# The token vector of the expert dots is read from two PSUM banks for three of the four token tiles; the merge and latent-head stages give up two PSUM banks each

## The chip, the cores and the metric

The kernel runs on one core of a Trainium2 chip. The metric is the device time of one execution in microseconds (us). The engines are named as in the profile: PE is TensorE (its weight loads are PEld), DVE is VectorE, ACT is ScalarE, POOL is GpSimd, SP is SyncE, which here only issues DMAs.

## The reference

Two transformer blocks over 512 tokens of width 1024. The first has a Mamba-2 scan, a short convolution, a merge of the two and a layer of 16,384 small experts; the second has two kinds of attention and an MLP. The expert layer is the part that the change touches:

```
def peer_ffn(h, w_q, sub_keys, expert_u, expert_v):
...
        u = expert_u[eidx]
        v = expert_v[eidx]
        act = jax.nn.gelu(jnp.einsum('td,thkd->thk', xb, u).astype(jnp.float32), approximate=False)
        return jnp.einsum('thk,thkd->td', (g * act).astype(v.dtype), v)
```

`eidx` holds 8 heads x 16 chosen experts per token. Per token, 128 rows of `peer_u` are each multiplied with the token's vector and summed (a dot), the 128 dots go through a gelu, and 128 rows of `peer_v`, each times its coefficient, are added up.

## The kernel before

The 512 tokens are four tiles of 128 tokens (one token on each of the 128 partitions), handled as two halves of two tiles. Block one (`project`, `scan`, `merge`, norm, `route`) runs for the first half and then for the second; block two (`mix_two`, `mlp_two`) follows. A stage ends when PE, DVE, ACT and SP have arrived at its barrier.

The experts are background work in class `Experts`. There are 1024 units in a fixed order: for each tile 128 dot units, then 128 add units. One unit is one row gather of 128 rows of 4 KB, one per token, 0.52 MB:

- POOL issues it (`indirect_dma_start`, L1254). It reads the 128 row numbers from the SBUF tile `chosen`, and the rows land in one of the 16 slots of the ring `expert_rows`. Before it issues unit n, POOL waits until unit n-16 has been used.
- A dot unit is used by DVE in one instruction (L1328): slot times token vector `u`, written back to the slot, with the sum along the row as accumulator output. Both inputs lie in SBUF.
- An add unit is used by DVE (L1338, slot times coefficient plus `h` or `u`), or, for some of them (`tensor_units`), by PE: a matmul with a diagonal matrix that adds up in the two PSUM banks `expert_sum` (L1288); DVE adds these to `h` at the tile's end (L1352).

Each foreground stage has a quota of units (`PLAN_ONE`, `PLAN_TWO`). DVE takes some between its own instructions (`bg.use`) and the rest of the quota after its last instruction of the stage (`bg.use_rest`), so a late gather holds up what stands behind it on DVE. Which tile runs where:

- dots of the first tile: `project` of the second half; its adds: `scan` of the second half
- dots of the second tile: `merge` of the second half, 54 of them at its start, then 6 or 4 after each DVE step; its adds: the end of `merge`, the norm, `route`
- dots of the third tile: norm, `project_two` (all 72 of its quota in `use_rest`, since DVE has nothing else there), `latent_heads` and the start of `attend`; its adds: `attend` to the first `norm_add`
- fourth tile: what follows, to the end of its adds in the first `mlp_two`

Weights come in slabs of 2 MB that SP loads into two buffers; the load of a slab waits until PE has used the one that lay there.

PSUM has eight banks. `expert_sum` is held in `scan`, `route` and from `attend` on. In `merge` four banks `y_turned` take first the transposes of y, then the gate products; ACT empties them. In `latent_heads` three banks `lat_turned` take transposes.

Of the kernel before, what the change touches and what calls it, by code (L numbers as in the profile page):

```python
# [15 lines left out]
ds = bass.ds  # L16
# [91 lines left out]
def _program(nc, t, out, top):  # L108
# [268 lines left out]
    with first:  # L377
# [38 lines left out]
        def block_one(half, buffers, lend, bg, plans):  # L416
# [56 lines left out]
            with ExitStack() as ctx:  # L473
# [20 lines left out]
        bg.start(0, u[0], part_h[0], chosen[0], weight[0], chosen_ready)  # L494
        block_one(1, [uT[:, i, 0:META + TOK - SC_TAPS + 1] for i in range(7)],
                  (part_h[1], tiles_of(u1[:])), bg, PLAN_ONE + (UNITS,))
        bg.start(1, u1, part_h[1], chosen1, weight1, chosen_ready)
# [6 lines left out]
    def mix_two(first, T, seen, now, plan, per, prepared=None):  # L504
# [4 lines left out]
        with ExitStack() as ctx:  # L509
# [38 lines left out]
            landed = [sem(f"out2_landed{i}", keep=True) for i in range(2)]  # L548
            if now and first == 0:
                now.share_with_tensor(ctx, psum)  # L550
            plan()
# [45 lines left out]
    with ExitStack() as ctx:  # L597
        plans = iter(PLAN_TWO + (2 * UNITS,))
        plan = lambda: bg.plan(next(plans))
        LAST = TT + 1  # L600
        seen = [keys_and_values(ctx)]
        with experts:
            mix_two(0, TT, seen, bg, plan, 3)
# [22 lines left out]
def project(frame, slab_loader, ident, uT, z, xs, xs_meta, bt, bt_meta, bf, cf, dt, constants, carry,  # L626
# [10 lines left out]
    with ExitStack() as ctx:  # L637
# [6 lines left out]
        turned = [psum(ctx, f"x_turned{i}", [P, NT, P]) for i in range(2)]  # L644
        turned_meta = [psum(ctx, f"x_turned_meta{i}", [P, 512]) for i in range(2)]
        dt_bank = turned[0][:].rearrange("p t c -> p (t c)")[:, 0:(TT + 1) * HEADS].rearrange(
# [274 lines left out]
def scan(frame, consts, z, xs, xs_meta, bt, bt_meta, bf, cf, dt, decays, state, rows, half, bg, scaling, gating=None):  # L921
# [12 lines left out]
    with ExitStack() as ctx:  # L934
# [8 lines left out]
        root, scale, root_ready, y_scaled = scaling  # L943
        if bg:
            bg.share_with_tensor(ctx, psum)
        sums = psum(ctx, "sums", [P, 512])
# [240 lines left out]
class Experts:  # L1187
# [15 lines left out]
    def __init__(self, nc, t, sem, ctx, block, ident):  # L1203
# [12 lines left out]
        self.tensor_units += [UNITS + n for n in range(SLOTS + 8, TO_ATTENTION) if n % 8 in self.IN_ATTENTION]  # L1216
        self.halves = []
        self.goal = self.done = self.active = self.diags = self.products = self.sums = self.base = 0

# [59 lines left out]
    def tensor_sums(self, pe, n):  # L1279

        end = self.by_tensor(min(self.base + n, self.goal))
        for k in range(self.products, end):
# [4 lines left out]
            for side in range(2):  # L1287
                ins = pe.matmul(self.total[side][:], self.diag[:, k % self.DIAGS, :],  # L1288
                                self.row(unit)[:, side * 512:(side + 1) * 512],
                                start=k == self.by_tensor(tile), stop=k == self.by_tensor(tile + SLOTS) - 1)  # L1290
# [49 lines left out]
    def _sum_up(self, dve, end, u, h):  # L1340
# [4 lines left out]
        if shared:  # L1345
# [4 lines left out]
            for side in range(2):  # L1350
                o = h[:, side * 512:(side + 1) * 512]
                ins = dve.tensor_tensor(o, o, self.total[side][:], ALU.add)  # L1352
        ins.then_inc(self.complete, 1)
# [6 lines left out]
def merge(frame, ident, uT, z, yT, gates, vT, h, small, half, bg, y_scaled, slab, landed, loaded):  # L1360
# [7 lines left out]
    with ExitStack() as ctx:  # L1368
# [54 lines left out]
        def _(pe):  # L1423
            enter(pe)
            def turn_y():

                pe.wait_ge(y_scaled, TT)
                for j in range(KI):
                    if j >= 4:
                        pe.wait_ge(turned_used, j - 3)  # L1430
                    for m in range(TT):
                        ins = pe.transpose(turned[j % 4][:, 0, m * P:(m + 1) * P], z[:, m, j * P:(j + 1) * P], ident[:])
                    ins.then_inc(turned_done, 1)
# [4 lines left out]
            for i in range(0, 2 if own_gates else 0):  # L1438
                for s in range(2):
                    pe.wait_ge(landed[s], i * 16 + 16)  # L1440
                    for q in range(2):
                        pe.wait_ge(gates_used, i * 4 + (2 * s + q + 1))
                        for j in range(2):
                            c = (2 * q + j) * P
                            for k in range(KD):
                                ins = pe.matmul(turned[2 * s + q][:, j, :], slab[s][:, k, c:c + P], uT[:, k, own],
                                                start=k == 0, stop=k == KD - 1)
# [49 lines left out]
        def _(act):  # L1497
# [3 lines left out]
            def drain_y():  # L1501
                for j in range(KI):
                    act.wait_ge(turned_done, j + 1)
                    act.activation(yT[:, j, :], turned[j % 4][:, 0, :], ACT.Copy,
                                   scale=gain[:, j:j + 1]).then_inc(turned_used, 1)
# [3 lines left out]
            for i in range(0, 2 if own_gates else 0):  # L1509
                for p_ in range(4):  # L1510
                    act.wait_ge(product, i * 4 + (p_ + 1))
                    act.activation(gates[i][:, ds(2 * p_, 2), :], turned[p_][:], ACT.Sigmoid
                                   ).then_inc(gates_used, 1)
# [79 lines left out]
def route(frame, slab_loader, ident, uT, slab, chosen, weight, room, count, bg,  # L1593
# [8 lines left out]
    with ExitStack() as ctx:  # L1602
# [19 lines left out]
        at = kept("best_at_float").bitcast(BF16)[:, 0:Q * TOPK]  # L1622
        if bg:
            bg.share_with_tensor(ctx, psum)
        product = [psum(ctx, f"q_product{i}", [P, 512]) for i in range(2)]
# [334 lines left out]
def latent_heads(frame, ident, eps, small, constants_in, latent, qbT, kbT, values, first, T, bg):  # L1960
# [10 lines left out]
    with ExitStack() as ctx:  # L1971
# [34 lines left out]
        def _(act):  # L2006
# [11 lines left out]
            for j in range(3):  # L2018
                act.wait_ge(turned_done, j + 1)
                act.activation(latT[:, j, :], lturn[j][:, 0:T, :].rearrange("p m c -> p (m c)"), ACT.Copy,  # L2020
                               scale=gain[:, j:j + 1]).then_inc(latT_ready, 1)
            act.wait_ge(reduced, 1)
# [90 lines left out]
        def _(pe):  # L2113
            enter(pe)
            pe.wait_ge(scaled, 2 * T)
            for j in range(3):
                for m in range(T):
                    ins = pe.transpose(lturn[j][:, m, :], normed[:, m, j, :], ident[:])
                ins.then_inc(turned_done, 1)
# [984 lines left out]
```

## Time and profile before

| | |
|---|---|
| device time, median of 3 runs | 2778.02 us (2776.9 to 2784.32) |
| span of the profiled execution, first to last instruction | 2853.2 us |
| the profiled execution's device time | not recorded apart from its span |
| busy: PE / DVE / POOL / ACT | 2357.0 / 1754.3 / 1247.8 / 576.5 us |
| DMA | 832.08 MB, mean 292 GB/s; 536.94 MB of it by POOL's gathers (q0) |

Busy times are sums of instruction durations. The POOL time is nearly all from the 1024 gather issues: an issue is busy on POOL until its descriptors are made, and the transfer itself comes later. The profiled execution was 75.2 us longer than the median run; durations and order are read from it, the time itself from the runs.

### The profile page before, as it was taken

To read this page: it belongs to the slowest core of one execution; us is meant where nothing else is said; L and a number is where in the kernel's file an instruction comes from. 1 tells how busy PE (TensorE), PEld (TensorE's weight loads), DVE (VectorE), ACT (ScalarE), POOL (GpSimd) and SP (SyncE) were. 2 spreads that over 40 slices of the span, in tenths; PEclk is the share of its full clock that TensorE was granted. 3 is DMA by queue.
4 is the path that set the end of the run, shared out by engine and by line. 5 is a ranking of instruction groups with operands and counts; after the bars stand their busy time and mean duration, and the time that the engine had idled before them with its cause. 6 is when DMAs were issued, how large, how long until landed. Compare 5 with 4: busy or idle time off the path is not lost. (4 is left out here: it accounts for less than half of the span.)

```text
span 2853.2 us, 28354 instructions
## 1 busy us (share of the span) xinstructions
PE 2357.0 (83%) x9768; PEld 1658.2 (58%) x9768; DVE 1754.3 (61%) x3620; ACT 576.5 (20%) x1562; POOL 1247.8 (44%) x1058
## 2 busy tenths in 40 slices
PE   7999999889774887799788766486497799999988
PEld 6847888565662555588454454234185455557765
DVE  3325420179998887486768876975868677741510
ACT  4421300111332221000112201231123211012321
POOL 0000000004887666477545576675566577710000
PEclk9998999999996888899899887698796899999999
DMA  4322243337999999999987999898899899973376
GB/s 153 148 105 79 97 150 145 140 118 305 411 412 322 364 360 379 363 403 415 415 323 245 332 364 365 318 354 319 347 414 380 327 414 414 414 284 126 130 282 227
DMA packets 187055, 832.08 MB, mean 292 GB/s; under 512 B 22417, under 2 KB 22673, under 8 KB 174113
## 3 DMA queue, kind: packets, MB, share of 16 engines
q0 software_dynamic: 147456, 536.94, 49.0%
q1 hardware_dynamic: 39456, 293.33, 26.3%
q8 instruction: 79, 1.29, 0.2%
q14 instruction: 64, 0.52, 0.1%
HBM read 828.09 MB, written 2.10 MB: 291 GB/s over the span
## 5 line engine op out<-in xcount | busy, mean ns | idle before, releaser
L1254 POOL DMA_INDIRECT expert_rows<-in_peer_u,chosen x512 | 660.0, 1289 | 985.2 <-DVE chosen L1839 641.0
L1254 POOL DMA_INDIRECT expert_rows<-in_peer_v,chosen x512 | 584.4, 1141 | 275.8 <-issue 140.7
L1328 DVE SCALAR_TENSOR_TENSOR expert_rows<-expert_rows,u 128x1024 f32<-128x1024 f32 x512 | 603.2, 1223 | 69.8 <-DMA expert_rows<-in_peer_u,chosen 43.8
L1338 DVE SCALAR_TENSOR_TENSOR h<-expert_rows,expert_coef,h 128x1024 f32<-128x1024 f32 x194 | 249.9, 1288 | 34.3 <-DMA expert_rows<-in_peer_v,chosen 26.2
L1338 DVE SCALAR_TENSOR_TENSOR u<-expert_rows,expert_coef,u 128x1024 f32<-128x1024 f32 x190 | 244.9, 1289 | 38.5 <-DMA expert_rows<-in_peer_v,chosen 32.5
L1288 PE MATMUL expert_sum<-expert_rows,expert_diag 128*128 128x512 f32 x496 | 241.6, 634 | 30.1 <-ACT expert_diag L1275 21.9
L2977 PE MATMUL mlp_up<-mlp_xT,mlp_slab 128*128 128x384 f32 (+1 forms) x1024 | 227.4, 384 | 1.3 <-ACTq L132 0.8
L2969 PE MATMUL mlp_down<-mlp_slab,upT 128*128 128x512 f32 x512 | 222.2, 592 | 0.0
L2977 PEld LDWEIGHTS mlp_up<-mlp_xT,mlp_slab 128*128 128x128 f32 x1024 | 158.1, 195 | 73.6 <-issue 5.7
L1288 PEld LDWEIGHTS expert_sum<-expert_rows,expert_diag 128*128 128x128 f32 x496 | 95.7, 203 | 137.9 <-issue 132.0
L2969 PEld LDWEIGHTS mlp_down<-mlp_slab,upT 128*128 128x128 f32 x512 | 96.7, 190 | 117.1 <-issue 115.3
L720 PE MATMUL product<-uT,expert_rows 128*128 128x272 f32 x512 | 121.5, 393 | 0.8 <-DMA expert_rows<-in_w_in 0.8
L720 PE MATMUL product<-uT,in_slab 128*128 128x256 f32 x512 | 114.6, 379 | 0.0
L1902 PE MATMUL in_product<-xT,in_slab 128*128 128x256 f32 x320 | 80.3, 400 | 38.4 <-issue 38.2
L720 PEld LDWEIGHTS product<-uT,expert_rows 128*128 128x128 f32 x512 | 95.3, 190 | 19.4 <-DVEq L132 0.9
L720 PEld LDWEIGHTS product<-uT,in_slab 128*128 128x128 f32 x512 | 95.4, 190 | 12.4 <-issue 0.5
L815 DVE SCALAR_TENSOR_TENSOR h<-h,conv_taps 128x272 f32<-128x272 f32 x96 | 48.2, 502 | 80.1 <-ACT h L788 77.9
L1902 PEld LDWEIGHTS in_product<-xT,in_slab 128*128 128x128 f32 x320 | 63.7, 200 | 55.3 <-issue 47.5
L3001 ACT ACTIVATE upT<-mlp_up 128x384 f32<-128x384 f32 (+1 forms) x64 | 24.6, 384 | 334.3 <-PE mlp_up L2977 321.7
L1456 PE MATMUL mix_product<-uT,expert_rows 128*128 128x258 f32 (+1 forms) x384 | 85.4, 386 | 5.1 <-ACTq L132 5.1
L1456 PE MATMUL mix_product<-uT,mix_slab 128*128 128x258 f32 (+1 forms) x384 | 84.0, 381 | 0.5 <-DVE u L1556 0.5
L1456 PEld LDWEIGHTS mix_product<-uT,expert_rows 128*128 128x128 f32 x384 | 74.1, 193 | 16.0 <-ACTq L132 5.2
(559 smaller groups left out, 3604.0 us busy)
## 6 DMA issues: line engine op xcount, KB each, us to landing
expert_rows<-in_w_in SPq DMA_DIRECT2D x27, 2048.0 KB, 7.4
in_slab<-in_w_in SPq DMA_DIRECT2D x22, 2048.0 KB
mlp_slab<-in_w_up SPq DMA_DIRECT2D x64, 512.0 KB, 6.1
mlp_slab<-in_w_down SPq DMA_DIRECT2D x64, 512.0 KB, 5.3
mix_slab<-in_w_in SPq DMA_DIRECT2D x10, 2048.0 KB
out_slab<-in_w_out SPq DMA_DIRECT2D x6, 2048.0 KB, 7.9
expert_rows<-in_ssd_w_out SPq DMA_DIRECT2D x4, 2048.0 KB, 8.0
expert_rows<-in_peer_w_q SPq DMA_DIRECT2D x4, 2048.0 KB, 9.7
```

The costliest lines, as they stand in the source:

```text
L720: ins = pe.matmul(bank[n % 4][:, 0:W], slab[s][:, k, c:c + P], uT[:, k, A:A + W], start=k == 0, stop=k == KD - 1)
L815: ins = dve.scalar_tensor_tensor(a, b[:, k:k + W], taps[:, n, k:k + 1], a, ALU.mult, ALU.add)
L1254: pool.indirect_dma_start(out=self.row(n), out_offset=None, in_=self.tables[0 if dot else 1], in_offset=bass.IndirectOffsetOnAxis(ap=picks ...
L1288: ins = pe.matmul(self.total[side][:], self.diag[:, k % self.DIAGS, :], self.row(unit)[:, side * 512:(side + 1) * 512], start=k == self.by ...
L1328: dve.scalar_tensor_tensor(self.row(n), self.row(n), 1.0, u, ALU.mult, ALU.mult, accum_out=dot).then_inc(self.rows_used, 1)
L1338: dve.scalar_tensor_tensor(o, self.row(n), coef, o, ALU.mult, ALU.add).then_inc(self.rows_used, 1)
L1456: ins = pe.matmul(pair[r % 2][:, j, 0:w], lhs(j, k), rhs(k), start=k == 0, stop=k == k_tiles - 1)
L1902: ins = pe.matmul(both[n % 4][:, j, :], lhs(j, k), xT[:, k, :], start=k == 0, stop=k == KD - 1)
L2969: ins = pe.matmul(down[2 * m + side][:], upT[:, n % (2 * PER), m * P:(m + 1) * P], as_down(i % R)[:, j, side * 512:(side + 1) * 512], star ...
L2977: ins = pe.matmul(bank[n % UPS][:, 0:W], slab[i % R][:, j, k, :], xT[:, k, :], start=k == 0, stop=k == KD - 1)
L3001: act.activation(o, bank[n % UPS][:, 0:W], ACT.Relu).then_inc(relu_done, 1)
```

## The change

- `expert_sum` becomes one PSUM tile of two banks. As before PE sums into its halves. In addition, as `near`, it holds the token vector of the tile whose dots are taken.
- At the first dot of a tile DVE copies `u` there (`_bring`: it waits until its own earlier uses have ended, copies, waits for the copy). The dots read `near` in place of `u`.
- The two banks are held through the whole second half of block one, and through the first `mix_two` (`share_with_tensor`); after that `end_share` sets `near` to None, and the fourth tile's dots read `u` in SBUF as before.
- `project` allocates its meta banks in the first half alone; `merge` in the second half has two `y_turned` banks in place of four; `latent_heads` packs its first two transposed tiles in one bank, and ACT waits for both before it reads the first.

```
+        with ExitStack() as ctx:
+            bg.share_with_tensor(ctx, psum)
+            block_one(1, ...)
...
+            with ExitStack() as shared:
+                bg.share_with_tensor(shared, psum)
+                mix_two(0, TT, seen, bg, plan, 3)
+            bg.end_share()
...
     def share_with_tensor(self, ctx, psum):
-        self.total = [psum(ctx, f"expert_sum{i}", [P, 512]) for i in range(2)]
+        both = psum(ctx, "expert_sum", [P, 2, 512])
+        self.total = [both[:, side, :] for side in range(2)]
+        self.near, self.held = both[:].rearrange("p a n -> p (a n)"), None
...
             if dot:
-                self._dot(dve, n, u[:, m, :], self.coef[:, m, at:at + 1])
+                if self.near is not None and self.held != (half, m):
+                    self._bring(dve, n, u[:, m, :])
+                    self.held = half, m
+                self._dot(dve, n, u[:, m, :] if self.near is None else self.near, self.coef[:, m, at:at + 1])
...
+    def _bring(self, dve, n, u):
+        if self.by_vector(n):
+            dve.wait_ge(self.rows_used, self.by_vector(n))
+        dve.tensor_copy(self.near, u).then_inc(self.brought, 1)
+        self.brings += 1
+        dve.wait_ge(self.brought, self.brings)
...
-        turned = [psum(ctx, f"y_turned{i}", [P, 2, TOK]) for i in range(4)]
+        TURNED = 2 if bg else 4
+        turned = [psum(ctx, f"y_turned{i}", [P, 2, TOK]) for i in range(TURNED)]
...
-                    if j >= 4:
-                        pe.wait_ge(turned_used, j - 3)
+                    if j >= TURNED:
+                        pe.wait_ge(turned_used, j - TURNED + 1)
...
-                        pe.wait_ge(gates_used, i * 4 + (2 * s + q + 1))
+                        n = i * 4 + 2 * s + q
+                        pe.wait_ge(gates_used, 4 - TURNED + n + 1)
...
-        lturn = [psum(ctx, f"lat_turned{i}", [P, NT, P]) for i in range(3)]
+        turned_two = [psum(ctx, f"lat_turned{i}", [P, 2, T * P]) for i in range(2)]
+        lturn = [turned_two[j // 2][:, j % 2, :] for j in range(3)]
...
-                act.wait_ge(turned_done, j + 1)
+                act.wait_ge(turned_done, 2 if j < 2 else 3)
```

DVE at the start of `project` of the second half, before (`expert_coef` is where a dot's sum goes):

```order
L801 UNCONDITIONAL_BRANCH
L1328 SCALAR_TENSOR_TENSOR expert_rows,expert_coef<-expert_rows,u 128x1024 x12
L815 SCALAR_TENSOR_TENSOR uT<-uT,conv_taps 128x256 x3
L1328 SCALAR_TENSOR_TENSOR expert_rows,expert_coef<-expert_rows,u 128x1024 x3
L815 SCALAR_TENSOR_TENSOR uT<-uT,conv_taps 128x256 x3
```

The same place in the changed kernel:

```order
L804 UNCONDITIONAL_BRANCH
L1340 COPY expert_sum<-u 128x1024
L1347 SCALAR_TENSOR_TENSOR expert_rows,expert_coef<-expert_rows,expert_sum 128x1024 x12
L818 SCALAR_TENSOR_TENSOR uT<-uT,conv_taps 128x256 x3
L1347 SCALAR_TENSOR_TENSOR expert_rows,expert_coef<-expert_rows,expert_sum 128x1024 x3
L818 SCALAR_TENSOR_TENSOR uT<-uT,conv_taps 128x256 x3
```

One copy is new, and the dots name `expert_sum` (PSUM) where they named `u` (SBUF); number and order are the same. Two more copies stand at the start of `merge` of the second half and in the norm at the start of the first `mix_two`.

PE in `merge` of the second half, at the change from the transposes of y to the gate products, before:

```order
L1432 MATMUL y_turned_340<-ident,z 128x128 x2
L1432 MATMUL y_turned_341<-ident,z 128x128 x2
L1446 MATMUL y_turned_338<-uT,mix_slab_331 128x256 x16
L1446 MATMUL y_turned_339<-uT,mix_slab_331 128x256 x16
L1446 MATMUL y_turned_340<-uT,mix_slab_332 128x256 x16
L1446 MATMUL y_turned_341<-uT,mix_slab_332 128x256 x16
```

and in the changed kernel:

```order
L1452 MATMUL y_turned_336<-ident,z 128x128 x2
L1452 MATMUL y_turned_337<-ident,z 128x128 x2
L1468 MATMUL y_turned_336<-uT,mix_slab_329 128x256 x16
L1468 MATMUL y_turned_337<-uT,mix_slab_329 128x256 x16
L1468 MATMUL y_turned_336<-uT,mix_slab_330 128x256 x16
L1468 MATMUL y_turned_337<-uT,mix_slab_330 128x256 x16
```

The same work goes through two banks by turns instead of four.

## Rows read from the trace of the kernel before

**Rows 1.** The page: costliest POOL and DVE groups; busy us, mean ns, idle before

```profile
L1254 POOL DMA_INDIRECT expert_rows<-in_peer_u,chosen x512 | 660.0, 1289 | 985.2 <-DVE chosen L1839 641.0
...
L1328 DVE SCALAR_TENSOR_TENSOR expert_rows<-expert_rows,u 128x1024 f32<-128x1024 f32 x512 | 603.2, 1223 | 69.8 <-DMA expert_rows<-in_peer_u,chosen 43.8
```

**Rows 2.** Timeline, POOL, dots back to back: start, us, engine, line, op

```profile
867.14 1.98 POOL L1254 DMA_INDIRECT expert_rows<-in_peer_u,chosen  x1 [0.30 <-issue]
```

**Rows 3.** Timeline, DVE, the same place

```profile
865.95 1.22 DVE L1328 SCALAR_TENSOR_TENSOR expert_rows<-expert_rows,u 128x1024 f32<-128x1024 f32 x1
...
867.09 1.22 DVE L1328 SCALAR_TENSOR_TENSOR expert_rows<-expert_rows,u 128x1024 f32<-128x1024 f32 x1
```

**Rows 4.** Timelines of DVE and POOL, 1226 to 1227 us

```profile
1226.25 0.68 DVE L1556 TENSOR_TENSOR u<-u,mix_product 128x512 f32<-128x512 f32 x1
...
1226.30 0.94 POOL L1254 DMA_INDIRECT expert_rows<-in_peer_u,chosen  x1 [0.30 <-issue]
```

**Rows 5.** Stretches: length, busy PE PEld DVE ACT POOL; PE clock, DMA share, GB/s

```profile
715.00:857.00 142.00, 105.86 (x508) 87.87 (x508) 139.51 (x260) 46.12 (x137) 115.17 (x89) 0.95 1.02 413
857.00:880.00 23.00, 0.00 (x0) 0.00 (x0) 22.82 (x42) 1.79 (x2) 19.65 (x12) 0.50 0.85 280
...
1611.00:1660.00 49.00, 42.00 (x170) 31.29 (x171) 44.20 (x80) 12.82 (x28) 36.29 (x23) 0.86 0.88 313
1660.00:1740.00 80.00, 41.59 (x143) 29.77 (x142) 61.84 (x103) 4.27 (x6) 61.59 (x56) 0.68 1.02 407
1690.00:1730.00 40.00, 9.86 (x17) 4.79 (x17) 30.68 (x51) 0.00 (x0) 30.30 (x29) 0.50 1.02 412
...
1825.00:1925.00 100.00, 74.08 (x233) 35.19 (x233) 78.95 (x158) 38.73 (x138) 77.11 (x67) 0.81 0.96 356
```

**Rows 6.** Timeline, PE, the end of `project_two`

```profile
1734.07 32.32 PE L1902 MATMUL in_product<-xT,in_slab 128*128 128x256 f32 x140 [0.63 <-issue]
```

**Rows 7.** Timeline, PE, `merge` of the second half after its gate products

```profile
1184.98 41.82 PE L1456 MATMUL mix_product<-uT,mix_slab 128*128 128x258 f32 x192
...
1355.67 29.20 PE L1490 MATMUL mix_product<-mix_slab,z 128*128 128x512 f32 x64 [2.86 <-DVE z L1575]
```

**Rows 8.** Groups of DVE and ACT instructions: busy us, mean ns, idle before

```profile
L1344 DVE TENSOR_TENSOR h<-h,u 128x1024 f32<-128x1024 f32 x4 | 4.9, 1225 | 0.1
...
L293 DVE TENSOR_SCALAR mix_normed<-x_in,mix_scale 128x1024 f32<-128x1024 f32 x4 | 3.0, 754 | 0.1
...
L1575 DVE TENSOR_TENSOR u<-u,gated 128x512 f32<-128x512 f32 x4 | 2.8, 691 | 0.1
...
L1572 DVE TENSOR_TENSOR gated<-h,mix_product 128x512 f32<-128x512 f32 x4 | 2.7, 687 | 22.7 <-PE mix_product L1456 22.7
...
L1504 ACT ACTIVATE yT<-y_turned,ssd_gain 128x256 f32<-128x256 f32 x16 | 6.3, 489 | 5.7 <-PE y_turned L1432 5.7
```

**Rows 9.** DVE's waits, 857 to 895 us: total, times, longest

```profile
DVE u L1336 <- DMA expert_rows<-in_peer_v,chosen: 2.8, 1, 2.8
DVE expert_rows L1328 <- DMA expert_rows<-in_peer_u,chosen: 1.2, 2, 0.8
DVE h L1338 <- DMA expert_rows<-in_peer_v,chosen: 0.8, 1, 0.8
```

**Rows 10.** The dots of 1602 to 1767 us, and the idle time ahead of them

```profile
L1328 DVE SCALAR_TENSOR_TENSOR expert_rows<-expert_rows,u x92: 1210/1224/1295, 1611.1 to 1749.2; 128x1024 f32<-128x1024 f32 x92
...
  DMA expert_rows<-in_peer_u,chosen: 17.9, 10
  issue: 4.0, 9
```

**Rows 11.** DVE's waits, 1801 to 1963 us (`attend`)

```profile
DVE u L1338 <- DMA expert_rows<-in_peer_v,chosen: 7.8, 6, 2.3
...
DVE h L1338 <- DMA expert_rows<-in_peer_v,chosen: 3.2, 3, 1.6
```

**Rows 12.** DMA queue of the weight slabs, 1240 to 1300 us: packets, MB, share

```profile
q1 hardware_dynamic: 576, 8.39, 33.1%
```

More of the change, by code:

```diff
@@ L494, in _program @@
         bg.start(0, u[0], part_h[0], chosen[0], weight[0], chosen_ready)
-        block_one(1, [uT[:, i, 0:META + TOK - SC_TAPS + 1] for i in range(7)],
-                  (part_h[1], tiles_of(u1[:])), bg, PLAN_ONE + (UNITS,))
+        with ExitStack() as ctx:
+            bg.share_with_tensor(ctx, psum)
+            block_one(1, [uT[:, i, 0:META + TOK - SC_TAPS + 1] for i in range(7)],
+                      (part_h[1], tiles_of(u1[:])), bg, PLAN_ONE + (UNITS,))
         bg.start(1, u1, part_h[1], chosen1, weight1, chosen_ready)
@@ L548, in mix_two @@
             landed = [sem(f"out2_landed{i}", keep=True) for i in range(2)]
-            if now and first == 0:
-                now.share_with_tensor(ctx, psum)
             plan()
@@ L644, in project @@
         turned = [psum(ctx, f"x_turned{i}", [P, NT, P]) for i in range(2)]
-        turned_meta = [psum(ctx, f"x_turned_meta{i}", [P, 512]) for i in range(2)]
+        turned_meta = [psum(ctx, f"x_turned_meta{i}", [P, 512]) for i in range(2)] if M else None
         dt_bank = turned[0][:].rearrange("p t c -> p (t c)")[:, 0:(TT + 1) * HEADS].rearrange(
@@ L943, in scan @@
         root, scale, root_ready, y_scaled = scaling
-        if bg:
-            bg.share_with_tensor(ctx, psum)
         sums = psum(ctx, "sums", [P, 512])
@@ L1217, in __init__ @@
         self.halves = []
+        self.near, self.brought, self.brings = None, sem("tokens_in_psum", keep=True), 0
         self.goal = self.done = self.active = self.diags = self.products = self.sums = self.base = 0
@@ L1263, in share_with_tensor, with end_share @@
     def share_with_tensor(self, ctx, psum):
-        self.total = [psum(ctx, f"expert_sum{i}", [P, 512]) for i in range(2)]
+        both = psum(ctx, "expert_sum", [P, 2, 512])
+        self.total = [both[:, side, :] for side in range(2)]
+        self.near, self.held = both[:].rearrange("p a n -> p (a n)"), None
+    def end_share(self):
+        self.near = None
     def diagonals(self, act, n):
@@ L1287, in tensor_sums @@
             for side in range(2):
-                ins = pe.matmul(self.total[side][:], self.diag[:, k % self.DIAGS, :],
+                ins = pe.matmul(self.total[side], self.diag[:, k % self.DIAGS, :],
                                 self.row(unit)[:, side * 512:(side + 1) * 512],
@@ L1351, in _sum_up @@
                 o = h[:, side * 512:(side + 1) * 512]
-                ins = dve.tensor_tensor(o, o, self.total[side][:], ALU.add)
+                ins = dve.tensor_tensor(o, o, self.total[side], ALU.add)
         ins.then_inc(self.complete, 1)
@@ L1428, in turn_y @@
                 for j in range(KI):
-                    if j >= 4:
-                        pe.wait_ge(turned_used, j - 3)
+                    if j >= TURNED:
+                        pe.wait_ge(turned_used, j - TURNED + 1)
                     for m in range(TT):
-                        ins = pe.transpose(turned[j % 4][:, 0, m * P:(m + 1) * P], z[:, m, j * P:(j + 1) * P], ident[:])
+                        ins = pe.transpose(turned[j % TURNED][:, 0, m * P:(m + 1) * P], z[:, m, j * P:(j + 1) * P],
+                                           ident[:])
                     ins.then_inc(turned_done, 1)
@@ L1445, in _ @@
                             for k in range(KD):
-                                ins = pe.matmul(turned[2 * s + q][:, j, :], slab[s][:, k, c:c + P], uT[:, k, own],
+                                ins = pe.matmul(turned[n % TURNED][:, j, :], slab[s][:, k, c:c + P], uT[:, k, own],
                                                 start=k == 0, stop=k == KD - 1)
@@ L1503, in drain_y @@
                     act.wait_ge(turned_done, j + 1)
-                    act.activation(yT[:, j, :], turned[j % 4][:, 0, :], ACT.Copy,
+                    act.activation(yT[:, j, :], turned[j % TURNED][:, 0, :], ACT.Copy,
                                    scale=gain[:, j:j + 1]).then_inc(turned_used, 1)
@@ L1511, in _ @@
                     act.wait_ge(product, i * 4 + (p_ + 1))
-                    act.activation(gates[i][:, ds(2 * p_, 2), :], turned[p_][:], ACT.Sigmoid
+                    act.activation(gates[i][:, ds(2 * p_, 2), :], turned[p_ % TURNED][:], ACT.Sigmoid
                                    ).then_inc(gates_used, 1)
@@ L1622, in route @@
         at = kept("best_at_float").bitcast(BF16)[:, 0:Q * TOPK]
-        if bg:
-            bg.share_with_tensor(ctx, psum)
         product = [psum(ctx, f"q_product{i}", [P, 512]) for i in range(2)]
@@ L2018, in _ @@
             for j in range(3):
-                act.wait_ge(turned_done, j + 1)
-                act.activation(latT[:, j, :], lturn[j][:, 0:T, :].rearrange("p m c -> p (m c)"), ACT.Copy,
-                               scale=gain[:, j:j + 1]).then_inc(latT_ready, 1)
+                act.wait_ge(turned_done, 2 if j < 2 else 3)
+                act.activation(latT[:, j, :], lturn[j], ACT.Copy, scale=gain[:, j:j + 1]).then_inc(latT_ready, 1)
             act.wait_ge(reduced, 1)
@@ L2117, in _ @@
                 for m in range(T):
-                    ins = pe.transpose(lturn[j][:, m, :], normed[:, m, j, :], ident[:])
+                    ins = pe.transpose(lturn[j][:, m * P:(m + 1) * P], normed[:, m, j, :], ident[:])
                 ins.then_inc(turned_done, 1)
```

1 line of the change is left out of this document (removed).

## The prediction

> **What bounds the kernel now.** I read the page first. No engine is busy all through: DVE has 61% of the span, and its costliest group is the dots; ahead of them it sat idle 69.8 us, 43.8 of that for gathered rows that had not landed. A gather's issue keeps POOL 1289 ns on average in the dots' half [rows 1]. That average is worth opening, so the timelines of POOL and DVE came next, where dots run back to back. An issue that starts at 867.14, 0.05 us into a dot, takes 1.98 us. The dot ends at 868.31, the issue at 869.12, 0.81 us later [rows 2, 3]. Dots follow each other every 1.14 us [rows 3], issues every 1.98 + 0.30 = 2.28 us, so one gather passes per two dots. The counter-example is an issue that starts 0.05 us into a DVE instruction which reads one operand from PSUM (`mix_product`) and the other from SBUF and writes SBUF: it takes 0.94 us [rows 4]. The reader is to see that the issue is held until a dot with two SBUF inputs has ended, and that 0.94 us is its own length.
>
> The Trainium skill, "SBUF — State Buffer", section "Who interferes with whom", says as much: a DVE instruction with two SBUF inputs contends with a GpSimd instruction that reads SBUF. The trace agrees (1.98 against 0.94 us).
>
> Next, where does a held issue cost anything? The stretches tell. In 715 to 857 us DVE is busy 139.5 of 142 us and the DMA engines move 413 GB/s: both are full, and quicker issues have nowhere to go. In 857 to 880 us it is 280 GB/s, in 1611 to 1660 us 313 GB/s, with POOL busy on 23 issues for 36.3 us. After that, 1660 to 1740 us, it is 407 GB/s again [rows 5]. I take 413 GB/s as a full DMA. In `merge` PE is the bound: from 1184.98 its matmul runs follow one another to 1384.9 (1355.67 + 29.20) with next to no gap, at most 2.86 us [rows 7], so DVE's waits there are paid from PE's slack.
>
> One stretch needs care. In 1690 to 1730 us PE has 17 records in 40 us, at half clock (0.50, 1.2 GHz), with the DMA full at 412 GB/s [rows 5]; the profile doesn't say why. At the pace of `merge`, 41.82 us for 192 records [rows 7], 17 records take 3.7 us, so some 36 us are stall. The profiled span is 75.2 us longer than the median run, so the timed runs can't hold all such stalls. PE ends `project_two` at 1766.4 in the profile [rows 6]; without 36 us of it that is 1730, ahead of the last dot of that quota at 1749.2 [rows 10]. In the timed runs I therefore take DVE, waiting for gathers, as what ends that stage. This is my choice; the profile alone says PE.
>
> **The change part by part.** The sum is of differences, and is taken from the median run, 2778.0; against the profile's span the same sum gives 2853.2 minus it, with `project_two` then in doubt.
>
> Dots themselves: 384 of 512 read PSUM. At 128x512 an instruction with one PSUM input takes 687 ns, one with both in SBUF 691 ns [rows 8]. I take 0 per dot.
>
> The Trainium skill, "VectorE: DVE Perf Modes", section on the TRN2 errata, speaks against the change: a fixed cost of 120 cycles from PSUM against 58 from SBUF, 62 cycles or 0.065 us at 0.96 GHz. By it the 384 dots would take an estimated 25 us more; rows 8 show nothing of the kind.
>
> Three copies of 128x1024 into PSUM: none is in the trace. Nearest are 754 ns (one input, SBUF to SBUF) and 1225 ns (two inputs) [rows 8]. PSUM as the output makes me take the upper one, with 0.1 for the two semaphore waits: 1.3 us. The first stands in `project`, where DVE is full, the third in the norm ahead of `project_two`, where PE waits for DVE: both are on the path. The second stands before 54 dots of `merge`, covered by PE's slack; without that cover it would be 1.3 more. Cost 2.6, between 1.5 and 4.
>
> Fewer banks: transposes in `merge` are paced by ACT's 16 copies of 489 ns [rows 8] with four banks or two; a gate product is 16 matmuls with two records each, 32 x 41.82/192 = 7.0 us [rows 7], far longer than ACT needs to empty a bank. `latent_heads` makes ACT wait for one more pair of transposes. Together 1 us, 0 to 2.
>
> End of the first tile's dots (857 to 895 us): DVE uses the last 23 dots back to back with POOL held on nearly each, uses up its lead, and then waits 2.8 + 1.2 + 0.8 = 4.8 us [rows 9]. With issues every 0.94 + 0.30 = 1.24 us against a dot every 1.14 the lead stays. What stands behind is the scan's own start on DVE. I take 3 gained, 0 to 4.8.
>
> Dots of the second tile (`merge`): PE-bound, 0, from 3 lost to 4 gained.
>
> Dots of the third tile (norm and `project_two`): 23 issues in 36.3 us would take 21.6. The DMA moved 313 GB/s in place of 413 for 49 us, a lack of 49 x (1 - 313/413) = 11.9 us [rows 5]. After it the DMA is full, so that this is all that can be given back, although DVE's waits sum to 17.9 + 4.0 = 21.9 us [rows 10]. I take 10, 0 to 12.
>
> Start of `attend`: the tile's last dots are still taken here, and the adds behind them run at 356 GB/s, not DMA-bound, with issues of 77.11/67 = 1.15 us on average [rows 5]. Adds have two SBUF inputs as before, so they go on holding POOL. But POOL comes to them with a fuller ring, and that can pay for part of DVE's waits of 7.8 + 3.2 = 11.0 us [rows 11]. I take 5, 0 to 11.
>
> The fourth tile isn't touched. Its adds end inside the first MLP.
>
> Sum: 3 + 10 + 5 - 2.6 - 1 = 14.4 us. **2778.0 - 14.4 = 2764 us.**
>
> **The rivals.**
> A, the issues get short, but the time is hidden. In the timed runs PE ends `project_two` after DVE, as in the profile, or the DMA is full a little later and nothing comes through: only the 3 us of 857 to 895 remain against 3.6 of cost, 2779 us. For it: PE's end at 1766.4, and 407 to 413 GB/s wherever the DMA was not starved. Against: the 75 us that the profile has too much.
> B, slower: the weight slabs pay. While gathers are queued, the slab queue gets 8.39 MB in 60 us, 140 GB/s [rows 12], so that a slab of 2.1 MB takes 15.0 us; PE uses one in 64 records, a third of the 192 in 41.82 us: 13.9 us [rows 7]. Today the gather queue thins out whenever POOL is held, and slabs catch up. If it never does, each of the 14 slabs from 1185 to 1385 us costs PE 1.1 us: 15 us, and with the other stages' gain lost 2778 + 15 + 3.6 - 3 = 2794 us. It decides once PE waits for slabs in more than that stage's odd tile. Against: the number of gathers per stage is fixed, and at 1240 to 1300 us the queues were full already while PE did not wait.
> C, a dot from PSUM is longer than one from SBUF. At 0.037 us per dot (14.4/384) the gain is gone, if all of it is on the path; at 0.05 us it is 19 us, 2783 us. Against: 687 against 691 ns, though these have half the length and no accumulator.
> D, the issue is held by the dot's write to SBUF or its accumulator, not by the second input; then only costs remain, 2782 us. Against: the instruction of rows 4 writes SBUF too. The Trainium skill's same SBUF section infers that making descriptors needs the write side alone, so that an instruction with two inputs wouldn't hold it; the trace disagrees, as shown.
>
> **How the numbers follow.** Forecast 0.60, A 0.22, B 0.10, C 0.05, D 0.03. A measurement of this kernel tells about 0.3%, 8.3 us, from no change. The forecast's own range runs from all upper gains at the lowest cost (4.8 + 4 + 12 + 11 - 1.5 = 30 us) to a small one, 2748 to 2775. Faster than 2769.7: 0.56 of the forecast, 0.03 of A. Slower than 2786.3: B's 0.10, 0.02 of C, 0.01 of D. The rest, 0.28, lies within. The range reaches from 2742, a little under the upper gains for a stage whose timed course I don't see, to 2784, which takes in A, C and D and leaves out B.
>
> **What would show it.** Issues in the dots of the first three tiles at 0.94 us, and as long as before in the fourth tile's; dots at 1.22; three copies between 0.75 and 1.3 us; over 390 GB/s where 280 and 313 stood; DVE's waits for `in_peer_u` rows before the fourth tile shorter. The forecast is wrong if PE shows waits for slabs in `merge` or `project_two` (B), if dots lengthen (C), if issues stay at 1.98 (D), or if all this comes out as said and the stages end when they did (A).

## The result and the profile after

| | before | after |
|---|---|---|
| device time, median | 2777.46 us (2774.11 to 2784.32, 4 runs) | 2752.68 us (2749.13 to 2757.73, 4 runs) |
| ratio after / before | | 0.9906, 95% interval 0.9885 to 0.9926 |
| span of the profiled execution | 2853.2 us | 2748.2 us, its device time 2750.07 |

The change gains 24.8 us; the forecast was 14.4. Timed again beside the later experiments the ratio was 0.9917 (0.9903 to 0.993). The profiled execution of after took 2.6 us less than the median of its runs, that of before 75 us more. A difference of these two profiles, 105 us, is therefore no measure of the change, and a second profile of the kernel before was taken first; what is compared below is that one (span 2775.4 us), unless the text says the first.

The page of after, costliest groups of POOL and DVE (busy us, mean ns, idle before), answers to [rows 1]:

```profile
L1256 POOL DMA_INDIRECT expert_rows<-in_peer_u,chosen x512 | 529.9, 1035 | 1040.9 <-DVE chosen L1859 640.5
...
L1347 DVE SCALAR_TENSOR_TENSOR expert_rows<-expert_rows,expert_sum 128x1024 f32<-128x1024 f32 x384 | 451.8, 1217 | 77.2 <-DMA expert_rows<-in_peer_u,chosen 72.4
...
L1347 DVE SCALAR_TENSOR_TENSOR expert_rows<-expert_rows,u 128x1024 f32<-128x1024 f32 x128 | 151.7, 1225 | 24.0 <-DMA expert_rows<-in_peer_u,chosen 17.3
```

A gather's issue in the dots' half is 0.25 us shorter on average than in the first profile of before (0.23 us than in the second, 1261 ns), and a dot from PSUM takes 1217 ns beside 1225 from SBUF in the same kernel. Back-to-back dots near 865 us, the place that [rows 2, 3] showed, POOL's timeline and then DVE's (start, us):

```profile
864.72 0.93 POOL L1256 DMA_INDIRECT expert_rows<-in_peer_v,chosen  x1 [0.30 <-issue]
865.96 0.94 POOL L1256 DMA_INDIRECT expert_rows<-in_peer_v,chosen  x1 [0.30 <-DVE expert_rows L1347]
```

```profile
864.72 1.22 DVE L1347 SCALAR_TENSOR_TENSOR expert_rows<-expert_rows,expert_sum 128x1024 f32<-128x1024 f32 x1
865.86 1.22 DVE L1347 SCALAR_TENSOR_TENSOR expert_rows<-expert_rows,expert_sum 128x1024 f32<-128x1024 f32 x1
```

Both issues start in the first 0.1 us of a dot, take 0.93 and 0.94 us, and end before the dot does. Of the 296 issues that start inside a dot of the first three tiles (inside means that the dot is what DVE began last) the longest takes 0.95 us. The like-for-like comparison is with issues that start in the first 0.3 us of such a dot: before, 93 of 106 take over 1 us, and the median of the 106 is 1.98; after, none of 95 does. The 83 inside dots of the fourth tile, which read `u` in SBUF, still go up to 1.99.

The three copies, in the answer for line 1340 (ns, least, median, most):

```profile
L1340 DVE COPY expert_sum<-u x3: 1220/1227/1228, 685.6 to 1561.7; 128x1024 f32<-128x1024 f32 x3
```

### The profile page after: what moved, and what is told of

Its sections match the earlier page's. It is cut to its first block and busy times, and to the rows that moved or that the text cites. A ratio compares the mean times of both kernels' runs of the same rounds, so it can differ in the third digit from the quotient of the medians.

```text
span 2748.2 us, 28360 instructions
## 1 busy us (share of the span) xinstructions
PE 2328.0 (85%) x9768; PEld 1645.1 (60%) x9768; DVE 1756.2 (64%) x3623; ACT 576.9 (21%) x1562; POOL 1102.6 (40%) x1058
## 5 line engine op out<-in xcount | busy, mean ns | idle before, releaser
L1256 POOL DMA_INDIRECT expert_rows<-in_peer_u,chosen x512 | 529.9, 1035 | 1040.9 <-DVE chosen L1859 640.5
L1256 POOL DMA_INDIRECT expert_rows<-in_peer_v,chosen x512 | 569.3, 1112 | 260.9 <-issue 126.6
L1347 DVE SCALAR_TENSOR_TENSOR expert_rows<-expert_rows,expert_sum 128x1024 f32<-128x1024 f32 x384 | 451.8, 1217 | 77.2 <-DMA expert_rows<-in_peer_u,chosen 72.4
L1296 PE MATMUL expert_sum<-expert_rows,expert_diag 128*128 128x512 f32 x496 | 235.1, 619 | 23.5 <-ACT expert_diag L1283 17.7
L1347 DVE SCALAR_TENSOR_TENSOR expert_rows<-expert_rows,u 128x1024 f32<-128x1024 f32 x128 | 151.7, 1225 | 24.0 <-DMA expert_rows<-in_peer_u,chosen 17.3
L1478 PEld LDWEIGHTS mix_product<-uT,mix_slab 128*128 128x128 f32 x384 | 75.8, 198 | 19.8 <-DVE sc_sx L1560 4.0
```

What stands on the lines that cost most here:

```text
L1256: pool.indirect_dma_start(out=self.row(n), out_offset=None, in_=self.tables[0 if dot else 1], in_offset=bass.IndirectOffsetOnAxis(ap=picks ...
L1296: ins = pe.matmul(self.total[side], self.diag[:, k % self.DIAGS, :], self.row(unit)[:, side * 512:(side + 1) * 512], start=k == self.by_te ...
L1347: dve.scalar_tensor_tensor(self.row(n), self.row(n), 1.0, u, ALU.mult, ALU.mult, accum_out=dot).then_inc(self.rows_used, 1)
L1478: ins = pe.matmul(pair[r % 2][:, j, 0:w], lhs(j, k), rhs(k), start=k == 0, stop=k == k_tiles - 1)
```

## The experiments

**1. The kernel before, profiled again.**

> The kernel before, unchanged, so that a second profile of it exists. Theory 1 (the first profile of it held stalls that the timed runs don't have): the span comes out near the timed median, 2770 to 2785 us, project_two of the first mix is 20 to 45 us shorter than its 145.5 us there, and the records of TensorE between 1690 and 1730 us don't thin out. Its idle time before the dots of tile three, 21.9 us, stays. Rival: the profiler always lengthens this kernel, then the span is again 2830 to 2870 us, although the changed kernel's profile had 2748.2 us against a median of 2752.7. Time: 1.000 times itself, within 0.3%.

Measured: 2776.72 us, ratio to itself 1.0003 (0.999 to 1.0017), span 2775.4. The first profile was long by 78 us: 25 in `scan` and 16 in `route` of the second half, 46 in `project_two`, of which `latent_heads` gave 32 back (the dots had caught up in the stall), 11 in `attend`, and about 3 in each of three others. Why is open; no later profile was like it. The timeline of PE and the stretches of before, second profile (length, busy PE PEld DVE ACT POOL; PE clock, DMA share, GB/s):

```profile
1659.66 12.47 PE L1902 MATMUL in_product<-xT,in_slab 128*128 128x256 f32 x57
1709.33 1.51 PE L2118 MATMUL lat_turned<-ident,latent_normed 128*128 128x128 f32 x6 [37.21 <-DVE latent_normed L2046]
```

```profile
1576.00:1626.00 50.00, 50.00 (x194) 38.26 (x194) 39.24 (x68) 5.21 (x10) 41.46 (x29) 0.92 0.87 298
1626.00:1672.00 46.00, 46.00 (x214) 40.28 (x212) 32.35 (x53) 3.58 (x6) 32.65 (x34) 1.00 1.02 415
```

and the same of after:

```profile
1659.72 11.82 PE L1922 MATMUL in_product<-xT,in_slab 128*128 128x256 f32 x54
1694.30 1.51 PE L2138 MATMUL lat_turned<-ident,latent_normed 128*128 128x128 f32 x6 [22.76 <-DVE latent_normed L2066]
```

```profile
1576.00:1626.00 50.00, 50.00 (x191) 38.04 (x191) 48.59 (x87) 5.21 (x10) 37.79 (x41) 0.92 1.02 411
1626.00:1672.00 46.00, 45.54 (x211) 39.74 (x210) 34.31 (x57) 4.01 (x7) 27.74 (x30) 1.00 1.02 414
```

This is the main reading of the case. The stall of PE in `project_two` [rows 5] is gone from both kernels: PE works through to 1672 us in each, busy for all of the first 50 us, so `project_two` ends when it did, and nothing is gained in it. The third tile's dots run beside it. With issues held, 29 pass in 50 us and the DMA moves 298 GB/s; unheld, 41 pass and it moves 411. What is behind comes out where PE first needs DVE again, at the transposes of `latent_heads`: PE sat idle 37.21 us ahead of them, and now 22.76, 14.5 us less. DVE gets to them only after its rest of the quota of `project_two`, which it uses after it has arrived at that stage's barrier (at 1591.5 us before, at 1590.2 after). The first of DVE's own instructions behind that rest, before and then after:

```profile
1707.93 0.17 DVE L2042 RECIPROCAL latent_scale<-latent_root 128x4 f32<-128x4 f32 x1
```

```profile
1692.73 0.17 DVE L2062 RECIPROCAL latent_scale<-latent_root 128x4 f32<-128x4 f32 x1
```

As expected were the span, a shorter `project_two` (by 46 us, where 20 to 45 was expected), PE's records, and that DVE's waits for rows of tile three stay: 23.2 us up to the end of `project_two`, 26.4 in all, where 21.9 had been up to the end of that stage.

The lengths of the stages of the second half and of the first mix, each from the last arrival at one barrier to the last arrival at the next, from the traces of before and after:

| | before | after | difference |
|---|---|---|---|
| `project` | 225.1 | 224.9 | -0.2 |
| `scan` | 212.7 | 207.6 | -5.1 |
| `merge` | 286.6 | 286.8 | 0.2 |
| `route` | 183.0 | 187.7 | 4.7 |
| `project_two` | 99.3 | 99.9 | 0.6 |
| `latent_heads` | 66.0 | 50.3 | -15.7 |
| `attend` | 150.7 | 138.4 | -12.2 |
| all the rest | 1551.7 | 1552.4 | 0.7 |

**2. What holds the issue: the write, or the second input?** First the banks of the changed kernel without its copies; every dot reads `u` in SBUF, and every second one writes to PSUM:

```
+        to_psum = self.near is not None and n % 2
+        if to_psum and self.by_vector(n) > 1:
+            dve.wait_ge(self.rows_used, self.by_vector(n) - 1)
-        dve.scalar_tensor_tensor(self.row(n), self.row(n), 1.0, u, ALU.mult, ALU.mult,
+        dve.scalar_tensor_tensor(self.near if to_psum else self.row(n), self.row(n), 1.0, u, ALU.mult, ALU.mult,
                                  accum_out=dot).then_inc(self.rows_used, 1)
```

> Banks as in the changed kernel, no copies, dots with both inputs in SBUF; in the first three tiles every second dot (the odd ones) writes its product, which nobody reads, to the two PSUM banks and not to the slot. Theory (the issue of a gather is held by the second SBUF input): issues that start inside either kind of dot last as long as before, up to 1.98 us, median 1.5 to 1.7, and end 0.81 us after the dot. Rival D (it is held by the write to SBUF): issues that start inside a dot that writes PSUM take 0.94 us, and only those inside the even dots are held.

Measured: 2776.42 us in one run beside 2775.56 of before. Timelines of DVE and POOL in this kernel:

```profile
689.79 1.23 DVE L1347 SCALAR_TENSOR_TENSOR expert_sum<-expert_rows,u 128x1024 f32<-128x1024 f32 x1
```

```profile
689.84 1.99 POOL L1256 DMA_INDIRECT expert_rows<-in_peer_u,chosen  x1 [0.30 <-issue]
```

The issue starts 0.05 us into a dot that writes PSUM and is held just as long, 1.99 us. Of 122 issues that start inside such dots 76 take over 1 us and end 0.80 us behind the dot; the median of all 122 is 1.62 us. Rival D falls for the write.

The second half of the question, with one SBUF input and the write left in SBUF (this kernel leaves out the product with `u`, so its dots have other values; gathers and order are the same):

```
-        dve.scalar_tensor_tensor(self.row(n), self.row(n), 1.0, u, ALU.mult, ALU.mult,
-                                 accum_out=dot)
+        dve.tensor_scalar(self.row(n), self.row(n), 1.0, 0.0, ALU.mult, ALU.add, accum_out=dot)
```

> The kernel before, with every dot replaced by an instruction with one SBUF input (slot times 1.0 plus 0.0, written back, with the accumulator output): the product with u is left out, no PSUM bank is touched by it. Theory (the second SBUF input holds the issue): all issues inside these take 0.94 us, those inside adds stay up to 1.98. Rival (an accumulator output, or a write to SBUF, holds it): up to 1.98 us as before. The time says little, since such an instruction may be shorter than a dot, 0.75 to 1.22 us.

The instruction turned out as long as a dot, so its time says more than expected: 2748.84 us, one run. The same two timelines:

```profile
863.23 1.21 DVE L1328 TENSOR_SCALAR_CACHE_REDUCE expert_rows<-expert_rows 128x1024 f32<-128x1024 f32 x1
```

```profile
863.26 0.94 POOL L1254 DMA_INDIRECT expert_rows<-in_peer_v,chosen  x1 [0.30 <-issue]
```

None of 383 issues inside these takes over 0.96 us, though they write SBUF and have an accumulator. `latent_heads` takes 50.5 us and `attend` 140.1, as in the changed kernel. So PSUM adds nothing of its own that these runs show; what counts is that one SBUF input is gone.

**3. Only the banks, and banks with copies.** In the first the call of `_bring` is taken out and the dots read `u`; in the second the copies are made and the dots read `u`:

```
-                self._dot(dve, n, u[:, m, :] if self.near is None else self.near, self.coef[:, m, at:at + 1])
+                self._dot(dve, n, u[:, m, :], self.coef[:, m, at:at + 1])
```

> The changed kernel with its banks (sharing, two banks less in merge and in latent_heads), but without the copies and with dots that read u in SBUF. Theory (the gain is the second SBUF input): the time of before, 2775 to 2781 us, fewer banks costing 0 to 2 us; issues inside dots as long as before. Rival (the gain comes from the banks or from where things lie): 2752 to 2765 us.

> The same, with the three copies made, but dots that still read u in SBUF. Theory: the copies cost 2.6 us over the kernel with the banks alone, between 1.5 and 4: 2777 to 2784 us. Each copy lasts 1.1 to 1.3 us. If a copy lasts 0.75 us, their cost is under 2 us and not to be told from nothing.

Measured: 2776.92 us, ratio 1.0007 (0.9994 to 1.002), and 2773.86 us, ratio 1.0001 (0.9987 to 1.0014). Neither can be told from the kernel before; the copies, 3.7 us of DVE time by their durations, are lost in the scatter of a median. Issues inside dots still go up to 1.99 us in both. The gain is in the operand. (In `latent_heads` the change gives up one bank, three to two, not two as the title and the expectation have it; `merge` gives up two.)

**4. One tile at a time.** `near` is used for one tile's dots alone:

```
+                near = self.near if (half, m) == (0, 0) else None
-                if self.near is not None and self.held != (half, m):
+                if near is not None and self.held != (half, m):
```

with (0, 1) for the second tile and (1, 0) for the third.

> The changed kernel, but with the copy and the PSUM operand for the dots of the first tile alone; the other dots read u in SBUF. Theory as forecast: scan of the second half ends earlier by 3 to 5 us (5.1 in the two profiles), less 1.2 of copy; merge is bound by TensorE and keeps that. Revised by the second profile of before: route gives these 5 us back (TensorE starts it at a lower clock), and the end of project_two is the same to 0.6 us, so 2773 to 2778 us. Rival (the first tile carries the gain through fuller rings): 2755 to 2765 us.

> The same for the dots of the second tile alone, which run in merge of the second half. Theory: TensorE bounds merge, 0 us, from 3 lost to 4 gained around the time of the kernel with the banks alone: 2773 to 2780 us, merge 286 to 288 us. Rival B (slabs pay while the gather queue is never thin): merge 290 to 300 us and the time above 2785 us.

> The same for the dots of the third tile alone. Theory: nearly the whole gain is here, 2750 to 2757 us, with latent_heads some 15 us and attend some 12 us shorter than the 66.0 and 150.7 us in the second profile of before. Rival (all three tiles share the gain as in the forecast, 3 of 18 us in the first): 2755 to 2765 us, with attend shorter by 5 us at most.

| PSUM operand for | median | ratio to before (95%) |
|---|---|---|
| first tile | 2773.84 us | 0.9989 (0.9976 to 1.0002) |
| second tile | 2780.54 us | 1.0007 (0.9993 to 1.0022) |
| third tile | 2756.17 us | 0.9926 (0.9902 to 0.9949) |
| all three (the change, timed again) | 2752.56 us | 0.9917 (0.9903 to 0.993) |

The third tile carries the gain, 21.8 us by its medians (20.6 by its ratio) of the 24.2 to 24.8 of the whole change. With the second tile alone `merge` takes 285.7 us, so rival B does not appear there. PE's timelines at the first transposes of `latent_heads`, third tile alone and then first tile alone:

```profile
1706.36 1.51 PE L2139 MATMUL lat_turned<-ident,latent_normed 128*128 128x128 f32 x6 [23.06 <-DVE latent_normed L2067]
```

```profile
1714.44 1.51 PE L2139 MATMUL lat_turned<-ident,latent_normed 128*128 128x128 f32 x6 [38.25 <-DVE latent_normed L2067]
```

With the third tile alone `latent_heads` takes 50.3 us and `attend` 139.7, with the first alone 66.8 and 144.6. The first tile gives 3 us by its ratio (7 to -1 by the interval), nothing that is certain: its own profile has `scan` at 214.9 us, longer than before. Over all kernels of this study `scan` of the second half took 207.5 to 216.4 us in no order (the first profile's 237.8 left out), so the 5.1 us of the table are within its scatter.

The same holds for a part of the 12.2 us of `attend`. Here are all profiles that have the quotas of before, again without the first, by what the third tile's dots read. Two SBUF inputs: the kernel before, the two of experiment 3, the one that writes PSUM, first tile alone, second tile alone. One: the changed kernel (twice), third tile alone, the one-input kernel of experiment 2.

| | two SBUF inputs, 6 profiles | one SBUF input, 4 profiles | difference of the means |
|---|---|---|---|
| `project_two` | 95.9 to 99.8, mean 98.6 | 97.6 to 99.9, mean 99.2 | 0.6 |
| `latent_heads` | 63.7 to 67.1, mean 65.6 | 50.3 to 52.5, mean 50.9 | -14.7 |
| `attend` | 144.6 to 151.2, mean 148.4 | 135.3 to 140.1, mean 138.4 | -10.0 |

In `latent_heads` and `attend` the two groups don't overlap. The means give 24.1 us, close to the 24.8 of the timed runs; the one pair of profiles gave 27.3 in the same stages.

**5. The quotas.** PE still waits 22.76 us for DVE in `latent_heads`. So 12 units of `project_two` were moved behind it, in both kernels to `merge_two`, and in the changed one also to `attend` instead:

```
-PLAN_TWO = (20, 72, 22, 86, 48, 8, 8, 36, 24, 10, 4, 3)
+PLAN_TWO = (20, 60, 22, 86, 60, 8, 8, 36, 24, 10, 4, 3)     to merge_two
+PLAN_TWO = (20, 60, 22, 98, 48, 8, 8, 36, 24, 10, 4, 3)     to attend
```

> The changed kernel, unchanged, timed beside the two below. 2748 to 2758 us, ratio 0.989 to 0.993. Its profile again has latent_heads at 50 us and attend at 138 to 140 us; scan of the second half anywhere from 207 to 216 us if its 5.1 us were scatter, 207 to 209 us if they belong to the change.

> The changed kernel with 12 units of the quota of project_two given to merge_two (72 and 48 become 60 and 60). Theory: DVE's rest of that quota, which runs on after TensorE has ended project_two, is what ends latent_heads, and merge_two has 26 us of idle DVE at its end: latent_heads 12 to 15 us shorter (12 dots of 1.22 to 1.28 us), some of it given back in attend, 2738 to 2745 us. Rival (TensorE's own work of latent_heads or the slabs end it once DVE is 5 us earlier, or attend takes all of it back): 2748 to 2755 us.

> The same quotas in the kernel before. Theory: it gains as much, 12 to 15 us, 2762 to 2768 us, and stays some 20 us behind the changed kernel with these quotas, since its dots still hold POOL. Rival (what the operand gives and what the quota gives are the same idle time of TensorE in latent_heads): it gains more than the changed kernel does, 20 us or over, and comes within 10 us of it.

> The changed kernel with 12 units of project_two's quota given to attend instead of merge_two (72 and 86 become 60 and 98). The sum of the first four quotas stays 200, so TensorE keeps its share of the third tile's adds, which it lost with the other plan. Theory: latent_heads 13.6 us shorter as there, DVE's 9.2 us of idle time at the start of merge_two pays for most of the units, and norm_add stays at 15.6 us: 2736 to 2743 us. Rival (VectorE has no such slack, whatever the stage the units are put in): 2744 to 2752 us.

| kernel | median | ratio to before (95%) |
|---|---|---|
| changed | 2752.56 us | 0.9917 (0.9903 to 0.993) |
| changed, 12 units to `merge_two` | 2745.51 us | 0.9893 (0.9878 to 0.9908) |
| changed, 12 units to `attend` | 2751.99 us | 0.9908 (0.9888 to 0.9928) |
| before, 12 units to `merge_two` | 2770.72 us | 0.998 (0.997 to 0.999) |

The changed kernel, profiled again here, has `latent_heads` at 52.5 us and `attend` at 135.3 (50 and 138 to 140 were expected) and `scan` at 207.5, which leaves open whether those 5.1 us are more than scatter.

PE at the transposes in the changed kernel with 12 units in `merge_two`:

```profile
1677.22 1.51 PE L2138 MATMUL lat_turned<-ident,latent_normed 128*128 128x128 f32 x6 [6.46 <-DVE latent_normed L2066]
```

`latent_heads` lost 13.6 us as expected, but about half came back. The expectation had taken DVE's arrival at the barrier of `merge_two`, 26 us ahead of PE's, for idle time. It is none: DVE goes on there with its rest of the quota. DVE's waits from 1895 to 1950 us show its one idle stretch in the changed kernel:

```profile
DVE post_mix_scale L2881 <- ACT post_mix_root L2869: 9.3, 1, 9.3
```

It is absent from the answer for the kernel with 12 units in `merge_two`, whose `norm_add` is 5.4 us longer: DVE makes 67 adds from `merge_two` to there instead of 54, since fewer adds fall to PE too. With the units in `attend` that stage is 8.6 us longer and `merge_two` 5.6, and of the 13.7 next to nothing is left; there the expectation missed altogether, and the rival held. DVE's busy time in `attend` had risen by 13 us (115.69 to 128.98). It looks as if DVE is the bound, or close to it, from `latent_heads` to `norm_add`. The kernel before gained 6 us from the same move, no more than the changed one, so that the two gains do not compete; the 12 to 15 us expected of it were missed for the same reason, with `latent_heads` 14.3 us shorter (51.7) and `norm_add` 6.8 longer (22.4). Best of the study by the median is the changed kernel with 12 units in `merge_two`, 7 us ahead of the changed one beside it; the intervals of their ratios just overlap.

## Why the forecast was right in kind and short in size

**Dots cost nothing from PSUM: right.** 1217 against 1225 ns. Rival C had no part. The larger fixed cost from PSUM that the Trainium skill states (page "VectorE: DVE Perf Modes", section on the TRN2 errata), by the prediction's estimate 0.065 us per dot, does not appear in these instructions, of which one input is in PSUM and the other in SBUF.

**The issue is held by a second SBUF input: right, and now shown** by experiments 2, one that moves the write away and one that takes the input away. The rule of the Trainium skill, "SBUF — State Buffer", section "Who interferes with whom", agrees with 0.94 against up to 1.99 us, also while the write is elsewhere, if the issue counts as an instruction that reads SBUF; its rows name `chosen`, the SBUF tile of the row numbers, as an input. The prediction went too far in saying that the trace disagrees with the page's inference that making descriptors needs only the write side: what is held may be the reading of the row numbers, and no run here separates the two.

**Copies 2.6 and banks 1: right as far as can be told.** A copy takes 1.23 us (1.3 taken). Of the 3.6 us taken for both, the kernel with both (experiment 3) shows somewhere between 3.9 us lost and 3.6 gained, by its interval.

**First tile, 3 (0 to 4.8): not settled.** Alone it gave 3 us, with an interval from 1 lost to 7 gained. The waits of 4.8 us [rows 9] were those of the first profile. In the second they are 1.6 us, so that there was less to give back:

```profile
DVE h L1338 <- DMA expert_rows<-in_peer_v,chosen: 1.0, 1, 1.0
DVE u L1336 <- DMA expert_rows<-in_peer_v,chosen: 0.6, 1, 0.6
```

**Second tile, 0: right.** `merge` is 286.6 and 286.8 us, DVE's waits for rows there 57.3 and 57.5 us, on PE's slack both times. Rival B had no part either: PE shows no wait for a slab there, nor in `project_two`.

**Third tile, 10 (0 to 12): the first term that was too small,** 14.7 measured as a mean (15.7 in the pair of profiles), above its upper bound. The forecast took the lack of bytes from 49 us that begin with the tile's first dot, 49 x (1 - 313/413) = 11.9 us, as the most that could come back. In the second profile the first dot is at 1563.0, and the starved stretch is from 1576 to 1626, deeper since the full queue of the first 13 us isn't in it: 50 x (1 - 298/413) = 13.9 us, and PE's idle time fell by 14.5. And the place was wrong: "in the timed runs I therefore take DVE, waiting for gathers, as what ends that stage". The order was right: DVE's last dot of that quota ends at 1707.9 us, PE at 1672.1. But the stage doesn't wait for these dots, since DVE arrived at the barrier at 1591.5 and used the rest behind it. So PE ends `project_two`, as rival A had it, but A's conclusion that the time is then hidden did not follow: DVE's rest runs on past the barrier and holds up PE in `latent_heads` instead.

**Start of `attend`, 5 (0 to 11): the second,** 10.0 measured as a mean, twice the term (12.2 in the pair of profiles). DVE's waits for rows of the third tile's adds, from the last dot to the first `norm_add`, before and then after:

```profile
DVE u L1338 <- DMA expert_rows<-in_peer_v,chosen: 12.7, 11, 2.6
DVE h L1338 <- DMA expert_rows<-in_peer_v,chosen: 10.7, 12, 1.3
```

```profile
DVE u L1357 <- DMA expert_rows<-in_peer_v,chosen: 7.5, 10, 1.6
DVE h L1357 <- DMA expert_rows<-in_peer_v,chosen: 6.2, 10, 1.3
```

They fell from 23.4 to 13.7 us. The forecast had only 11.0 us of such waits to give back [rows 11], because the first profile had fewer of them. The mechanism is the one it named: POOL issues the first of these rows 21.8 us ahead of DVE's first add (1737.8 and 1759.6 us), where it had been 13.2 (1762.7 and 1775.9), and that lead is used up over the stage. That DVE sets the pace of `attend` was not in the forecast: ACT waited 75.3 us there for `att_bias` from DVE, and waits 60.3 now, besides some 16 us ahead of the first one in both kernels (before, then after).

```profile
ACT probs L2623 <- DVE att_bias L2697: 42.4, 14, 4.7
ACT probs L2623 <- DVE att_bias L2700: 32.9, 15, 6.0
```

```profile
ACT probs L2643 <- DVE att_bias L2717: 31.4, 13, 4.3
ACT probs L2643 <- DVE att_bias L2720: 28.9, 14, 6.1
```

So the sum of 14.4 lacked 4.7 and 5.0 us in two terms; with 24.7 in place of 15 it comes to 24.1, or to 21.1 without the 3 of the first tile, which are not shown. The interval of the measured gain is 20.6 to 31.9 us. That the time lay inside the stated range (2742 to 2784) is in part luck: its lower end had room for 4.8 us from the first tile, which are uncertain, and for 4 from the second, which alone gave at most 2 by its interval, and the third tile's excess over its own bound used that room.

## What to carry to other kernels

Look at how long a DMA issue on GpSimd takes inside each kind of VectorE instruction: where it grows with the number of SBUF inputs and the DMA is not full, moving one shared input to PSUM feeds the queue, at no cost per instruction here. The gain shows not where the queue was starved but where the next engine first waits for the consumer, so follow the late work past the stage's barrier, and count an engine's rest behind the barrier before its slack is spent. And if a profiled execution is longer than the timed ones by more than the effect, take a second profile before working out terms from it.

## What was not expected of the hardware

- One execution of the kernel before ran 78 us longer than a second profiled one, at the same program, with PE stalled at half clock for some 36 us [rows 5] while DMA was full. No run shows the cause.
- The granted clock in the first 20 us of `route` of the second half differed from kernel to kernel, 0.96 before, 0.88 with the banks alone and 0.84 after, and with it the stage, 183.0, 186.3 and 187.7 us. It does not follow the change: with 12 units in `attend` it was 0.95 and the stage 183.1 us, and with the second tile alone 0.84 and 188.2 us. PE also waited 2.2 us there for a row before and 4.5 after; which is the cause of which is open. The rows of before and of after (PE clock is the third figure from the end):

```profile
1370.90:1390.90 20.00, 16.45 (x76) 13.26 (x76) 19.75 (x17) 4.57 (x11) 14.72 (x16) 0.96 1.02 408
```

```profile
1365.00:1385.00 20.00, 14.42 (x58) 10.69 (x59) 19.78 (x17) 3.62 (x8) 14.73 (x16) 0.84 1.01 408
```

- An operation with one SBUF input, a scalar pair and an accumulator took 1215 ns at 128x1024 (in the kernel with one SBUF input), as long as one with two inputs, while the first add of a tile, one input and no accumulator, took 745 ns.
